# One core, a long block kernel: seven-product layer's two ends re-ordered, and one slab first at the outset

## The reference

```python
h = x
h = h + hybrid_mixer(rmsnorm(h, mix_norm), w_in, ...)     # outset: its first products are "z0"
h = h + memory_cross_attention(rmsnorm(h, xattn_norm), ..., w_o)   # its last product is "wo"
gate, up = jnp.split(rmsnorm(h, ffn_norm) @ w_gate_up, 2, axis=-1) # the "seven-product layer"
h = h + (jax.nn.silu(gate) * up) @ w_down                  # "dn"
# second block
mod = silu(c) @ ada_w[layer] + ada_b[layer]                # done beside the seven-product layer
```

## Time and profile before

| | us |
|---|---|
| median of 3 runs | 2929.49 (2929.01 to 2931.03) |
| the profiled execution | 2931.55 |
| its span, first to last instruction | 2929.7 |
| PE busy in it | 2814.9 (96%) |
| DVE, ACT, POOL busy | 1872.1, 1297.8, 723.1 |

### The profile page before, as it was taken

How to read it: one execution, slowest core, us unless ns; L and a number is a source line. 1 busy time by engine, 2 the same in 40 slices (tenths; PEclk the granted TensorE clock), 3 DMA queues, 4 the chain that set the end, 5 groups by cost and what they waited for, 6 DMA issues and landing times.

```text
span 2929.7 us, 37370 instructions
## 1 busy us (share of the span) xinstructions
PE 2814.9 (96%) x14198; PEld 2349.2 (80%) x14198; DVE 1872.1 (64%) x2550; ACT 1297.8 (44%) x2086; POOL 723.1 (25%) x925
## 2 busy tenths in 40 slices
PE   8999999999999999999999999999999899999998
PEld 6878787778887788887888678788888777888986
DVE  6564475764455788887334736789878745318974
ACT  5321347432444322222211435678767624427851
POOL 0000003300002566663000011456545300004520
PEclk9999999999999999999999999999999999999999
DMA  4111333232311344446311323100001231131032
GB/s 142 58 43 52 129 107 128 98 115 87 100 58 47 115 148 141 146 148 225 109 48 46 112 65 88 49 1 12 12 15 37 101 108 44 51 94 64 18 116 72
DMA packets 201521, 245.46 MB, mean 84 GB/s; under 512 B 11776, under 2 KB 152320, under 8 KB 199808
## 3 DMA queue, kind: packets, MB, share of 16 engines
q1 hardware_dynamic: 184320, 186.37, 20.0%
q0 software_dynamic: 9104, 28.32, 3.2%
q10 hardware_dynamic: 7920, 28.38, 2.9%
HBM read 192.11 MB, written 46.20 MB: 81 GB/s over the span
## 4 chain that ended last, share of the span: by engine, by line
PE 84%; DVE 7%; ACT 3%; POOL 2%; issue 2%; DMA 1%; SPq 0%; ACTq 0%; DVEq 0%; POOLq 0%
PE P L348 46%; PE P L289 5%; PE P L291 5%; PE P L290 5%; PE P L286 5%; PE P L2713 4%; PE P L317 2%; PE P L2727 2%; PE P L2726 1%; PE P L1111 1%; PE P L1585 1%; PE P L3319 1%; POOL T L2975 1%; POOL WS L3456 1%; DVE WST L3431 1%
## 5 line engine op out<-in xcount | busy, mean ns | idle before, releaser
L273 DVE TENSOR_TENSOR wl<-wf,wh 128x1024 fp32r<-128x1024 f32 (+3 forms) x163 | 192.7, 1182 | 665.5 <-ACT wh L265 665.0
L265 ACT ACTIVATE wh<-wf 128x1024 fp32r<-128x1024 f32 (+3 forms) x163 | 166.9, 1024 | 766.2 <-PE P L348 703.0
L348 PE MATMUL P<-XH,wh 128*128 128x512 f32 (+1 forms) x1232 | 385.0, 394 | 6.8 <-DVE TMP L1388 2.5
L348 PE MATMUL P<-XL,wh 128*128 128x512 f32 (+1 forms) x1232 | 381.7, 391 | 0.0
L348 PE MATMUL P<-XH,wl 128*128 128x512 f32 (+1 forms) x1232 | 380.6, 390 | 0.0
L2975 POOL TENSOR_TENSOR T<-T,WST 128x512 f32<-128x512 f32 x256 | 260.9, 1040 | 220.3 <-DVE WST L2945 197.5
L348 PEld LDWEIGHTS P<-XH,wh 128*128 128x128 f32 (+1 forms) x1232 | 229.0, 187 | 62.2 <-issue 12.7
L348 PEld LDWEIGHTS P<-XH,wl 128*128 128x128 f32 (+1 forms) x1232 | 230.2, 187 | 51.1
L348 PEld LDWEIGHTS P<-XL,wh 128*128 128x128 f32 (+1 forms) x1232 | 229.9, 187 | 51.2
L289 PE MATMUL P<-FO,U 128*128 128x512 f32 x616 | 242.5, 394 | 8.0 <-DVE U L1833 6.7
L290 PE MATMUL P<-FO,U 128*128 128x512 f32 x616 | 240.7, 391 | 0.0
(11 more groups left out here) (483 smaller groups left out, 6281.3 us busy)
## 6 DMA issues: line engine op xcount, KB each, us to landing
AW<-ada_t POOLq DMA_DIRECT2D x96, 256.0 KB, 3.4
wf<-gu_units SPq DMA_DIRECT2D x88, 256.0 KB, 3.0
H<-scratch_h SPq DMA_DIRECT2D x32, 512.0 KB, 6.5
wf<-w_in SPq DMA_DIRECT2D x28, 512.0 KB, 3.8
scratch_h<-H SPq DMA_DIRECT2D x24, 512.0 KB, 5.9
scratch_g<-T ACTq DMA_DIRECT2D x22, 512.0 KB, 3.0
scratch_f<-T ACTq DMA_DIRECT2D x22, 512.0 KB, 3.2
wf<-odd_w_in SPq DMA_DIRECT2D x20, 512.0 KB, 3.8
```

Source lines behind the costliest of these rows:

```text
L265: e.activation(self.sb["wh"][i % 2][:, 0:m], self.sb["wf"][i % 2][:, 0:m], ACT.Copy).then_inc(*self.s.w_hi.up(i))
L273: e.tensor_tensor(l, f, h.bitcast(F32), ALU.subtract).then_inc(*self.s.w_lo.up(i))
L348: ins = e.matmul(self.P[slot][0:m, t:t1], w, x[:, k, t:t1], start=first and k == 0, stop=last and k == kb - 1)
```

## The change

Four things are done:

- At the outset the order of loads is slab 0, block 0 of x, vectors, slab 1, blocks 1 to 3, constants, blocks 4 to 7. ACT and DVE split slab 0, then block 0, then slab 1. `pe_first_pair` waits for a slab at that slab's first step. The waits for the constants move to the roots.
- Pair 3's scaling and `form_sums` go ahead of unit 2's halves and of the last square, the sums on DVE in place of POOL. POOL prepares unit 3 with the first three; unit 3's halves are made between the two pieces of pair 3's forms.
- The norm's roots are taken after unit 2, and the two spreading matmuls follow unit 5 and product 3 of unit 6, into the seventh bank. ACT's and DVE's norm, `silu`, `product` and `store` of pair 0 shift to units 6 to 8. The 96 reductions are spread over units 10 to 84, not 6 to 87.
- At the end SP issues blocks 0 to 2 ahead of `dn`'s second slab, and DVE splits blocks 3 to 6 ahead of the last two drains.

The diff:

```diff
...
     def pe_first_pair(self, e, stage, xh, xl, ready, emptied, between):
...
             slots.append(self.tiles[stage, j][0])
-            e.wait_ge(*self.s.w_hi.to(i))
-            e.wait_ge(*self.s.w_lo.to(i))
-            self.pe_place(e, slots[j])
         kb = self.order[self.no[stage, 0]].shape[1]
...
         for j, k in steps:
+            if k == 0:
+                e.wait_ge(*self.s.w_hi.to(self.no[stage, j]))
+                e.wait_ge(*self.s.w_lo.to(self.no[stage, j]))
+                self.pe_place(e, slots[j])
             if j == 0:
...
     def sp_start(self, e):
+        x = lambda j: e.dma_start(self.H[:, j, :], self.dr["xT"][:, j, :]).then_inc(*self.s.h[j].up("x"))
+        self.sp_weights(e, 1)
+        x(0)
         e.dma_start(self.sb["vecs"][:, :], self.dr["vecs"]).then_inc(*self.s.vecs.up("in"))
+        self.sp_weights(e, 2)
+        for j in range(1, 4):
+            x(j)
         e.dma_start(self.sb["consts"][:, :], self.dr["consts"]).then_inc(*self.s.consts.up("in"))
-        self.sp_weights(e, 2)
-        for j in range(8):
-            e.dma_start(self.H[:, j, :], self.dr["xT"][:, j, :]).then_inc(*self.s.h[j].up("x"))
+        for j in range(4, 8):
+            x(j)
     def act_start(self, e):
+        self.act_weights(e, 0)
         e.wait_ge(*self.s.vecs.to("in"))
-        e.wait_ge(*self.s.consts.to("in"))
-        e.activation(self.sb["identr"][:, :], self.con("ident"), ACT.Copy).then_inc(*self.s.act.up("identr"))
-        self.act_weights(e, 0)
-        self.act_weights(e, 1)
         for k in range(8):
...
                          scale=self.vec("mix_norm", k)).then_inc(*self.s.hi.up(("raw", k)))
+            if k == 0:
+                self.act_weights(e, 1)
             self.act_square(e, "n0", k, self.H[:, k, :])
+        e.wait_ge(*self.s.consts.to("in"))
+        e.activation(self.sb["identr"][:, :], self.con("ident"), ACT.Copy).then_inc(*self.s.act.up("identr"))
     def dve_start(self, e):
+        self.dve_weights(e, 0)
         e.wait_ge(*self.s.vecs.to("in"))
-        e.wait_ge(*self.s.consts.to("in"))
-        self.dve_weights(e, 0)
-        self.dve_weights(e, 1)
         for k in range(8):
...
                                    op1=ALU.subtract).then_inc(*self.s.lo.up(("raw", k)))
+            if k == 0:
+                self.dve_weights(e, 1)
             self.dve_square(e, "n0", k)
-    def pe_start(self, e):
-        e.wait_ge(*self.s.vecs.to("in"))
         e.wait_ge(*self.s.consts.to("in"))
-        e.wait_ge(*self.s.act.to("identr"))
     def pe_z0(self, e):
-        between = {0: lambda e: self.pe_roots(e, "n0", self.T[2], self.s.dve.to(("n0", "sum", 7))),
-                   1: lambda e: self.pe_spread(e, "n0", self.T[2])}
+        def roots(e):
+            e.wait_ge(*self.s.consts.to("in"))
+            e.wait_ge(*self.s.act.to("identr"))
+            self.pe_roots(e, "n0", self.T[2], self.s.dve.to(("n0", "sum", 7)))
+        between = {0: roots, 1: lambda e: self.pe_spread(e, "n0", self.T[2])}
         self.pe_linear(e, "z0", self.sb["RAWH"], self.sb["RAWL"],
...
     def act_xattn_out(self, e):
...
         e.wait_ge(*self.s.hi.to(("form", p, piece)))
-        e.wait_ge(*self.sums_of(p).to(("t", p, 1)))
+        e.wait_ge(*self.s.dve.to(("t", p, 1)))
         e.tensor_tensor(lo, x, hi.bitcast(F32), ALU.subtract).then_inc(*self.s.lo.up(("form", p, piece)))
...
         def empty(e, j):
-            e.wait_ge(*self.s.dve.to(("h2", j)))
             if j == 7:
...
                 self.act_form(e, 2, 1)
+                e.wait_ge(*self.s.mm.to(("wo", 7)))
+                self.act_scaled(e, 3, 0)
+                self.act_scaled(e, 3, 1)
+                self.act_unit(e, 2)
+            e.wait_ge(*self.s.dve.to(("h2", j)))
             self.act_square(e, "n3", j, self.H[:, j, :])
...
             if j == 7:
-                e.wait_ge(*self.s.mm.to(("wo", 7)))
-                self.act_scaled(e, 3, 0)
-                self.act_scaled(e, 3, 1)
-                self.act_unit(e, 2)
                 self.act_form(e, 3, 0)
+                self.act_unit(e, 3)
                 self.act_form(e, 3, 1)
...
     def dve_xattn_out(self, e):
...
                 self.dve_form(e, 2, 1)
+                self.form_sums(e, 3)
+                self.dve_unit(e, 2)
             self.dve_square(e, "n3", j)
...
                 p = j // 2
-                self.form_sums(e, self.s.dve, p)
+                self.form_sums(e, p)
                 self.dve_form(e, p, 0)
...
                 self.dve_unit(e, 1)
-                self.form_sums(e, self.s.dve, 2)
+                self.form_sums(e, 2)
             if j == 7:
-                self.dve_unit(e, 2)
                 self.dve_form(e, 3, 0)
+                self.dve_unit(e, 3)
                 self.dve_form(e, 3, 1)
...
     def ada_unit(self, h):
-        return 6 + h * (UNITS - 6) // 96
+        return 10 + h * (UNITS - 13) // 96
...
     def sp_ffn(self, e):
...
         first = self.no[("dn", 0), 0]
-        for n in range(2):
-            e.wait_ge(*s.w_lo.to(("u", UNITS - 2 + n)))
-            self.sp_weights(e, first + n + 1)
+        e.wait_ge(*s.w_lo.to(("u", UNITS - 2)))
+        self.sp_weights(e, first + 1)
         for b in range(15):
...
                 e.wait_ge(*s.mm.to(self.unit_done(UNITS - {0: 4, 3: 3, 7: 1}[b])))
+            if b == 3:
+                e.wait_ge(*s.w_lo.to(("u", UNITS - 1)))
+                self.sp_weights(e, first + 2)
             if b == 7:
...
     def pool_ffn(self, e):
-        for u in range(3):
+        for u in range(4):
             self.pool_unit(e, u)
-        self.form_sums(e, self.s.pool, 3)
         e.wait_ge(*self.s.mm.to(("wo", 7)))
...
         self.pool_ada(e, 1)
-        for u in range(3, UNITS + 3):
+        for u in range(4, UNITS + 3):
             if u < UNITS:
...
     def pe_ffn(self, e):
...
         s = self.s
-        spare = self.bank_of(7)
         for u in range(UNITS):
...
                     elif i == 7:
+                        e.wait_ge(*s.dve.to(("n3", "root")))
+                    elif i == 14:
                         e.wait_ge(*s.act.to(("n3", "r", 1)))
...
                     ins.then_inc(*s.mm.up(("unit", u)))
-                if u == 3 and a in (0, 3):
-                    h = a // 3
-                    e.wait_ge(*s.dve.to(("n3", "diag")))
-                    if h:
-                        e.wait_ge(*s.act.to(("n3", "r", 0)))
-                    e.matmul(spare, self.con("ones"), self.T[2][:, self.half_of(h)], start=True,
-                             stop=True).then_inc(*s.mm.up(("n3", "spread", h)))
-            if u == 1:
+                if (u, a) in ((5, 6), (6, 3)):
+                    h = a == 3
+                    e.wait_ge(*(s.act.to(("n3", "r", 0)) if h else s.dve.to(("n3", "diag"))))
+                    if h == 0:
+                        count, key = self.drained(6)
+                        e.wait_ge(*count.to(key))
+                    e.matmul(self.bank_of(6), self.con("ones"), self.T[2][:, self.half_of(h)], start=True,
+                             stop=True).then_inc(*s.mm.up(("n3", "spread", int(h))))
+            if u == 2:
                 e.wait_ge(*s.dve.to(("n3", "sum", 7)))
                 for c in range(8):
-                    ins = e.matmul(spare[:, c:c + 1], self.T[2][:, 128 * c:128 * c + 128], self.con("ones")[:, 0:1],
-                                   start=True, stop=True)
+                    ins = e.matmul(self.bank_of(7)[:, c:c + 1], self.T[2][:, 128 * c:128 * c + 128],
+                                   self.con("ones")[:, 0:1], start=True, stop=True)
                 ins.then_inc(*s.mm.up(("n3", "roots")))
...
     def act_ffn(self, e):
...
             m, k = u // 4, u % 4
-            if u:
+            if u > 1:
                 self.act_unit(e, u + 2)
...
                 self.act_roots(e, "n3", self.bank_of(7)[:, 0:8], 0, D, s.mm.to(("n3", "roots")))
-            if u == 3:
-                e.wait_ge(*s.mm.to(("n3", "spread", 0)))
-                e.activation(T[3][:, 0:512], self.bank_of(7), ACT.Copy).then_inc(*s.act.up(("n3", "r", 0)))
-            if k == 0 and m:
+            if u == 6:
+                for h in range(2):
+                    e.wait_ge(*s.mm.to(("n3", "spread", h)))
+                    e.activation(T[3][:, self.half_of(h)], self.bank_of(6), ACT.Copy).then_inc(*s.act.up(("n3", "r", h)))
+                silu(0)
+            if k == 0 and m > 1:
                 silu(m - 1)
-            if k == 2 and m:
+            if u == 8:
+                store(0)
+            if k == 2 and m > 1:
                 store(m - 1)
...
                 e.activation(T[0][:, 0:512], self.gu_bank(m, 0), ACT.Copy).then_inc(*s.act.up(("p1", m)))
-            if u == 3:
-                e.wait_ge(*s.mm.to(("n3", "spread", 1)))
-                e.activation(T[3][:, 512:1024], self.bank_of(7), ACT.Copy).then_inc(*s.act.up(("n3", "r", 1)))
-            if u == 5:
+            if u == 9:
```

(21 more changed lines are left out.)

## The result

The changed kernel takes 2913.94 us (median of 4 runs, 2912.92 to 2915.24) against 2929.25 for the kernel before beside it: ratio 0.9949, 95% interval 0.9934 to 0.9963. It is faster by 15.3 us; the forecast was 22.1. The profiled execution took 2912.97 with a span of 2911.1. Two executions of kernels further down, one of e5 (5885.64) and one of e6 (5674.67), took about twice as long and are in no ratio; without them the two medians are 2913.29 and 2926.23.

What follows compares the result with a forecast made beforehand. PE, busy nearly throughout, was taken to lose time mainly at the outset, unit 3 and dn. Terms -2.2 - 12.8 + 0.3 - 7.4 = -22.1 us took 2929.49 to 2907.4; forecast 2904.5 to 2911 (63%), range 2904 to 2914.

Steps and rivals of the forecast that it cites:

- What bounds the kernel: Whole kernel: PE's largest idle entries sit in the three places the change touches: outset, unit 3, where dn begins.
- The outset: First products: slab 0 leads the loads, so PE starts at 9.7 us, not 11.9; -2.2 us (0.9 to 2.8).
- The rival with the clock: Outset: half pace ends at about 17 us whenever PE begins, gaining only 1.1 us; 2908.5, chance 14%.
- The start of the layer: Seven-product layer, units 0 to 8: -15.8 for the stretch, +1.7 spreading, +0.8 and +0.5 waits for c12; sum -12.8 us.
- Then the drains: Units 4 and 8: the drains come from an undelayed layer, so PE waits for c12, +0.8 and +0.5 us.
- by the rows' medians: Layer start, 941 to 951: few DVE steps are stretched by POOL's sums, though the contention rule would stretch each that meets them.
- The reductions: Layer: 96 reductions over 75 units, not 82; DVE has 2.7 us free per pair; +0.3 us (-1 to +3).
- slower rival: Whole layer: denser reductions make DVE the bound and push every c12 behind its product; 22 us eaten, chance 3%.
- The rival at 2913: Layer start: contention stretches DVE's chain from 931 to 945, making unit 3 and c12(0) late; +6 us, chance 12%.
- dn: After unit 87: earlier loads and splits of blocks leave no wait at dn's start; -7.4 us (-5 to -7.7).
- the thinnest cover: dn: slab 2 split at 1386.9, asked for at 1387.6; each microsecond later costs one.

Runs made afterwards that it cites:

- e5: The changed kernel with a third buffer for the reductions' operand, so each load is issued one reduction earlier; 2913.7 us.
- e6: The kernel before with only the outset's part of the change (order of loads and first splits, waits of `pe_first_pair`); 2927.02 us.
- e3: The changed kernel with each reduction cut to 8 of its 512 columns, all DMAs, waits and places kept; 2907.62 us.
- e2: The changed kernel with the reductions spaced as before (units 6 to 87) and the silu of c back in unit 5; 2911.75 us.
- e13: The changed kernel with a third buffer, and POOL issuing each reduction load one unit later, behind the next unit's sums; 2908.09 us.

## Why the prediction was wrong, point by point

- **What bounds the kernel.** The earlier trace rows are six lines of a longer list. Seven more stand between 11.9 and 3.5 us, the first of them 7.4, 7.1, 6.5 and 5.3, in places that the change doesn't touch, so "the largest entries sit in the three places" was not so. The terms don't rest on it.
- **The outset: -2.2, measured -3.5.** The right mechanism, undersized. 2.8 of it is the start: slab 0 was split from 4.78, where I took 5.0, and its table load lay ahead of it, hidden; `RAWL` began at 7.67, not 8.3. The rest is that PE stood at half pace for 4.4 us (9.10 to 13.50) and not for some 5.5, and that part is luck: in the sixteen traces with the new outset PE begins between 9.0 and 9.8, but full pace comes anywhere from 13.0 (e5) to 15.2 (e3).
- **The rival with the clock falls.** It had full pace at about 17 us whenever PE begins; it came by 15.2 in every trace with the new outset, and at 17.2 to 18.9 in the three with the old one. The Trainium skill (TensorE: Matmul & The Clock Gate, section Part 1: The HAM clock gate) says that the window runs freely; the traces agree in so far as the end is not at a fixed distance from the first matmul. What sets it in one execution stays open.
- **The start of the layer: -12.8, measured about -10.4.** DVE's chain held: form 2 at 926.72, sums of 0.68, unit 2's low half at 933.16, roots at 939.27, no wait at units 2 and 3. The step that was off is "Then the drains": the first ones began at 947.44, 1.4 later than forecast (950.3 less the 4.3 by which unit 0 came earlier). PE waited 1.38 for c11 in unit 4, where I had priced only c12 (0.42), and 0.23 and 0.38 in unit 8. With what the lists leave out (last section) unit 4 takes 2.4 us more than a unit's 4.76 and unit 8 1.2 (first matmuls at 945.87 and 953.05, at 969.14 and 975.08), where I had +0.8 and +0.5. Unit 4's sums were the late ones: two of them took 1.30 and 1.97 on POOL beside DVE's halves of unit 3 and of form 3, in place of 0.46, and ACT's high half waited 4.99 for them:

```profile
937.87 1.30 POOL L1820 TENSOR_TENSOR wf<-wf 128x128 f32<-128x128 f32 x1
939.13 1.97 POOL L1822 TENSOR_TENSOR wf<-wf 128x128 f32<-128x128 f32 x1
...
941.67 0.95 ACT L1833 ACTIVATE U<-wf 128x896 fp32r<-128x896 f32 x1 [4.99 <-POOL wf L1824]
```

  The Trainium skill's rule that the prediction cited (GPSIMD Engine Reference, section Key points: the two engines contend) agrees with these rows; I had set it aside "by the rows' medians".
- **The reductions: +0.3, measured about 6.5** (the shift goes from -14.8 at 1004 to -8.4 at the end of unit 87), outside its bounds of -1 and +3. This is the step that failed. It counted DVE's busy time per pair (2.7 us free, 0.36 more needed) and the units with two reductions ahead of c12. Both counts are right (DVE is busy 305.01 of 360.00 us in the window above) and neither is the limit: with POOL freed, DVE does the same work in the same order and S is 414.58. The limit was that DVE, POOL and ACT wait for one another in a ring. The trace of before showed it between 1000 and 1340, and I had read only PE's and DVE's waits:

```profile
POOL AW L1847 <- DVE MOD L1859: 86.1, 60, 2.3
```

  My slower rival named the right place, but put its price on busy time. The rival at 2913, "the wait moves to DVE's queue", has nearly the measured time and only by coincidence: its chain from 931 to 945 held, and the delays in units 4 and 8 explain 2.3 us of its 6.
- **dn: -7.4, measured -7.7** (shift -8.4 at the end of unit 87, -16.1 at 1474). No wait is left; `p1(21)` at 1358.67, blocks 3 to 6 from 1362.79, and slab 2, "the thinnest cover", split at 1374.96, 4.5 us before tile 1 ended at 1379.4.
- **The slack that the spacing buys.** I costed the spacing as a loss of 0.3 and didn't count what it holds off: with the old one the third slab is 2.9 late (e2).

What stays open: why the untouched stretches drift by 1 to 3 us from one execution to another, and what of the 6.7 us of S between the changed kernel and e13 goes by the slab's load and what by the drains; I didn't part these two.

## What to carry to other kernels

Before making side work denser, follow its whole loop, not its engine's busy time: who waits for it to be done, and what stands behind that waiter in its queue. A DMA issue that must wait for a consumer belongs behind the work that other engines need, and it needs one buffer more to stand there; either alone can be worth nothing or be much worse (here the buffer alone gives 2913.7, the place alone 2941.4, both 2908.1). When waits at one line grow, the line tells where the delay surfaces; moving work around at that line cost 28 us here, because the delay came by another engine.

## What the runs showed of the hardware

- A POOL sum of 128x128 takes 0.46 us alone and up to 1.45 (1193.48) while DVE's product of two 128x1024 operands runs (1.49 from 1193.12), three times as long; two at the layer's start took 1.30 and 1.97. A reduction of DVE's goes from 0.74 to 0.95 beside POOL's sums (1194.54).
- At the outset the granted clock reads 1.00 in windows both ahead of and behind 13.5 us, though two matmuls take 1.06 before it and 0.62 after. Pace there is read from durations only.
- With PE begun at 9.0 to 9.8 us, the half pace ends at 13.0 to 15.2 from one execution to the next (sixteen traces).
- Listed PE waits understate a stall: a matmul is shown with 0.39 to 0.50 us, but they start 0.227 apart (4.76 us for 21), so each event hides 0.2 to 0.3. In unit 8 of the changed kernel two listed waits sum to 0.61 us, and the unit takes 5.94 in place of 4.76.
